# Differential attention scores as 96-row single-pass products, stacked by GpSimd's DMA queue

## What is computed

```
proj = einsum('bsd,de->bse', h, w_in[l])
q = proj[..., :512].reshape(B, S, 8, 2, 32)      # 8 heads, 2 components c, 32 wide
k = proj[..., 512:1024].reshape(B, S, 8, 2, 32)
s = einsum('bqhcd,bkhcd->bhcqk', q, k) * 32 ** -0.5 - slope[h] * |i - j|
p = softmax(s, axis=-1)
a = p[:, :, 0] - lam * p[:, :, 1]
o = einsum('bhqk,bkhd->bqhd', a, v)              # then normed, gained, projected by w_o
```

## Time and profile before

| | us |
|---|---|
| median of 3 runs | 933.48 |
| lowest and highest | 933.23, 933.65 |
| span of the profiled execution (first to last instruction) | 931.5 |
| attention stage, layer 0, from the first side piece to the last PV product of the heads | 366.6 to 419.8 |
| the same, layer 1 | 660.0 to 713.2 |

### The profile page before, as it was taken

The page is one execution under the profiler, slowest core; times in us unless marked ns, Lnnn a source line. Parts: engine busy times, 40 slices in busy tenths (PEclk is TensorE's granted clock), DMA queues, the critical chain, the costliest instruction groups (busy, mean ns, idle before and its releaser), DMA issues.

```text
span 931.5 us, 13488 instructions
## 1 busy us (share of the span) xinstructions
PE 910.4 (98%) x4978; PEld 766.7 (82%) x4978; DVE 606.7 (65%) x1071; ACT 473.2 (51%) x764; POOL 123.3 (13%) x100
## 2 busy tenths in 40 slices
PE   9999999999999999999999999999999999999996
PEld 6999878889888869887888888877978788888885
DVE  4898677676768586767664545567486965545445
ACT  5855757466686444762543443424574354334430
POOL 5643863102000010002000000000001100000001
PEclk9999999999999999999999999999999999999998
DMA  9655232663533118232475555444432265455521
GB/s 354 229 183 169 95 126 86 220 232 137 185 132 136 57 61 346 91 115 112 158 260 181 181 197 201 172 154 158 160 136 91 96 228 214 174 192 180 186 85 45
DMA packets 22235, 151.72 MB, mean 163 GB/s; under 512 B 2592, under 2 KB 2976, under 8 KB 4256
## 3 DMA queue, kind: packets, MB, share of 16 engines
q1 hardware_dynamic: 20160, 142.62, 42.6%
q10 hardware_dynamic: 2016, 8.29, 2.5%
HBM read 149.85 MB, written 1.05 MB: 162 GB/s over the span
## 4 chain that ended last, share of the span: by engine, by line
PE 86%; DVE 7%; issue 2%; ACT 2%; POOL 1%; DMA 1%; POOLq 0%; DVEq 0%; ACTq 0%; SPq 0%
PE ps L492 15%; PE ps L494 15%; PE ps L498 15%; PE ps L1091 5%; PE ps L523 3%; PE ps L527 3%; PE ps L525 3%; PE ps L767 2%; PE ps L769 2%; PE ps L768 2%; PE ps L543 2%; PE ps L663 2%; PE ps L1109 2%; PE ps L666 1%; PE ps L665 1%
## 5 line engine op out<-in xcount | busy, mean ns | idle before, releaser
L1275 ACT CAST whi<-raw 128x2048 fp32r<-128x2048 f32 (+1 forms) x127 | 241.2, 1906 | 146.1 <-PE ps L498 112.5
L1740 DVE TENSOR_TENSOR wlo<-raw,whi 128x1024 fp32r<-128x1024 f32 x127 | 166.9, 1314 | 139.9 <-ACT whi L1275 139.4
L492 PE MATMUL ps<-whi,ahi 128*128 128x512 f32 (+2 forms) x448 | 173.6, 387 | 0.9 <-issue 0.6
L494 PE MATMUL ps<-wlo,ahi 128*128 128x512 f32 (+2 forms) x448 | 171.7, 383 | 0.0
L498 PE MATMUL ps<-whi,alo 128*128 128x512 f32 (+2 forms) x448 | 170.7, 384 | 0.0
L1746 DVE TENSOR_TENSOR wlo<-raw,whi 128x1024 fp32r<-128x1024 f32 x106 | 129.2, 1219 | 0.0
L492 PEld LDWEIGHTS ps<-whi,ahi 128*128 128x128 f32 x448 | 84.1, 188 | 18.5 <-issue 2.5
L494 PEld LDWEIGHTS ps<-wlo,ahi 128*128 128x128 f32 x448 | 84.2, 188 | 16.4 <-issue 0.5
L498 PEld LDWEIGHTS ps<-whi,alo 128*128 128x128 f32 x448 | 84.1, 188 | 16.4
L523 PE MATMUL ps<-ahi,whi 128*128 128x256 f32 x256 | 73.2, 286 | 0.0
L525 PE MATMUL ps<-alo,whi 128*128 128x256 f32 x256 | 72.4, 283 | 0.0
(11 more groups left out here) (282 smaller groups left out, 1708.8 us busy)
## 6 DMA issues: line engine op xcount, KB each, us to landing
raw<-in_wstream SPq DMA_DIRECT2D x134, 1024.0 KB, 4.8
par<-in_params ACTq DMA_DIRECT2D x5, 1024.0 KB, 4.7
tab<-in_tables ACTq DMA_DIRECT2D x1, 1370.0 KB, 9.5
res<-in_x SPq DMA_DIRECT2D x2, 512.0 KB, 4.5
out<-res SPq DMA_DIRECT2D x4, 256.0 KB, 2.0
par<-in_params ACTq DMA_DIRECT2D x1, 512.0 KB, 3.6
arena<-in_wf ACTq DMA_DIRECT2D x2, 256.0 KB, 5.1
arena<-in_wsmall ACTq DMA_DIRECT2D x1, 256.0 KB, 8.5
```

Source lines behind the costliest of these rows:

```text
L492: pe.matmul(banks[b][:, 0:cw], h_, wh[:, i, c], start=st, stop=False, skip_group_check=True)
L494: pe.matmul(banks[b][:, 0:cw], h_, wl[:, i, c], start=False, stop=False, skip_group_check=True)
L1275: act.copy(whi[:, u % SPL, c], raw[:, u % RAW, c]).then_inc(w_hi, 1)
L1740: dve.tensor_tensor(wlo[:, u % SPL, c], raw[:, u % RAW, c], whi[:, u % SPL, c].bitcast(F32), ALU.subtract).then_inc(w_lo_v, 1)
```

## The change

Each of the four bank images of queries and keys is now kept as a high part and a low part, both in the arena: ACT writes the high part as fp32r (`qk_out`, one instruction each instead of two for queries), and DVE the low part, bank minus high part (`qk_lo`, new, 128x512, four per layer). POOL then issues three DMAs per head (`stack_head`, new) which put three 32-row blocks on top of each other in a ring buffer of three places: rows 0 to 31 high queries and high keys, rows 32 to 63 low queries and high keys, rows 64 to 95 high queries and low keys. One product of 96 rows in fp32r then gives all three terms, so a head has four single-pass products and no float32 ones. The three places are the first half of `bhi`, the first half of `blo`, and `wst`, all idle then.

The order moves as well: the first scores come after 16 side pieces instead of 3, and `side_pieces` becomes 20, 26, 32 for h = -1, 0, 1 where it was 12, 22, 32. On DVE the split of the unit `vu 2` moves behind `qk_lo(2)`, `qk_lo(1)` goes behind `combine(0)`, and `qk_lo(3)` behind `combine(1)`. A bank is free for the next pieces only after its low part too (`qk_done` is now counted by DVE). Scores of component 0 are handed to DVE before those of component 1 are made, and each bank has its own wait. The columns of the weights are put in another order on the host, as are the scales.

```diff
-    return (0, 12, 22, 32, 36, 40, 44)[h + 2] if h < 5 else 48
+    return (0, 20, 26, 32, 36, 40, 44)[h + 2] if h < 5 else 48
+FIRST_SCORES = 16
+STACKED = ((0, 0), (1, 0), (0, 1))
+RING = 3
...
                 def diff_scores(h):
                     if h == 0:
-                        pe.wait_ge(qk_done, 4 * l + 2)
                         pe.wait_ge(cw_done, 3 * l + 3)
-                    if h == NH // 2:
-                        pe.wait_ge(qk_done, 4 * l + 4)
-                    if h >= 1:
-                        pe.wait_ge(ds_max, 2 * NH * l + 2 * h)
-                    for t in range(T):
-                        for c in range(2):
-                            n = 2 * h + c
-                            rr = slice(n % 4 * HD, (n % 4 + 1) * HD)
-                            mm = pe.matmul(X[c][:, t * S:(t + 1) * S],
-                                           qkt[rr, n // 4, t * P:(t + 1) * P], qkt[rr, 4 + n // 4, :],
+                    pe.wait_ge(stacked[h % RING], stack_uses(l, h))
+                    rows_ = slice(0, HD * len(STACKED))
+                    q_, k_ = (stack[h % RING][rows_, s, :, :] for s in range(2))
+                    for c in range(2):
+                        if h >= 1:
+                            pe.wait_ge(ds_max, 2 * NH * l + 2 * h - 1 + c)
+                        for t in range(T):
+                            mm = pe.matmul(X[c][:, t * S:(t + 1) * S], q_[:, c, t * P:(t + 1) * P], k_[:, c, :],
                                            start=True, stop=True, skip_group_check=True)
-                            if t == T - 1:
-                                mm.then_inc(ds_psum, 1)
+                        mm.then_inc(ds_psum, 1)
...
-                for n in range(3):
+                for n in range(FIRST_SCORES):
                     side_piece(n)
                 diff_scores(0)
...
-                for i in QK_ORDER[:2]:
-                    split.until(("qk", l, i))
+                def qk_lo(i):
+                    j = QK_ORDER.index(i)
+                    dve.wait_ge(qk_hi, 4 * l + j + 1)
+                    bank, hi, lo = G[j % 2], qk_part(i, 0), qk_part(i, 1).bitcast(F32R)
+                    if i < 2:
+                        ins = dve.scalar_tensor_tensor(lo, bank, const("q_scale")[:, i:i + 1], hi, ALU.mult,
+                                                       ALU.subtract)
+                    else:
+                        ins = dve.tensor_tensor(lo, bank, hi, ALU.subtract)
+                    ins.then_inc(qk_done, 1)
+                split.until(("qk", l, 0))
+                qk_lo(0)
+                qk_lo(2)
+                split.until(("qk", l, 2))
...
                         combine(h)
-
+                    if h == 0:
+                        qk_lo(1)
+                    if h == 1:
+                        qk_lo(3)
...
+            def stack_head(l, h):
+                if h == 0:
+                    pool.wait_ge(qk_done, 4 * l + 2)
+                if h == NH // 2:
+                    pool.wait_ge(qk_done, 4 * l + 4)
+                if h >= RING:
+                    pool.wait_ge(ds_psum, 2 * NH * l + 2 * (h - RING) + 2)
+                m, at_ = h % 4, qks_at[h // 4]
+                for b, (fq, fk) in enumerate(STACKED):
+                    first, step_ = 512 * fq, 1024 + 512 * (fk - fq)
+                    src = arena[m * HD:(m + 1) * HD, at_ + first:at_ + first + 2 * step_]
+                    pool.dma_start(stack[h % RING][b * HD:(b + 1) * HD, :, :, :].rearrange("p s c t -> p s (c t)"),
+                                   src.rearrange("p (s x) -> p s x", s=2)[:, :, 0:512]
+                                   ).then_inc(stacked[h % RING], 16)
```

More of the change, by code:

```diff
@@ L193 @@
                   ("cos_s", T * S), ("sin_s", T * S), ("cos_c", P), ("nsin_c", P), ("inv", HR),
-                  ("q_scale", 4), ("ident2", 32)):
+                  ("q_scale", 2), ("ident2", 32)):
     TAB[_name] = (TAB_W, TAB_W + _w)
@@ L254, in build, with qk_part @@
         FB = [G[0], G[1], X[0], X[1]]
+        def qk_part(i, low):
+            at_ = qks_at[i % 2] + (2 * (i // 2) + low) * 512
+            return arena[:, at_:at_ + 512]
         def acc_bank(n, t, b):
@@ L330, in build @@
         rtmp = arena[:, 12800:13312]
-        qkt = arena[:, 0:2048].rearrange("p (k c) -> p k c", k=8)
+        qks_at = (0, 10240)
+        stack = [s_.rearrange("p k c -> p (k c)").rearrange("p (s c t) -> p s c t", s=2, c=2)
+                 for s_ in (bhi[:, 0:4, :], blo[:, 0:4, :], wst[:, :, :])]
         v2 = arena[:, 2048:3072].rearrange("p (t c) -> p t c", t=T)
@@ L388, in build @@
         r_final = sem("r_final")
-        qk_done, v_done, u_done = (sem("qk_done"), sem("v_done"), sem("u_done"))
+        qk_hi, qk_done, v_done, u_done = sem("qk_hi"), sem("qk_done"), sem("v_done"), sem("u_done")
+        stacked = [sem(f"stacked{r}") for r in range(RING)]
         ds_psum, ds_max, dp_done, da_done = sem("ds_psum"), sem("ds_max"), sem("dp_done"), sem("da_done")
@@ L399, in build, with stack_uses @@
         out_sent = sem("out_sent")
+        def stack_uses(l, h):
+            return 16 * len(STACKED) * (l * len(range(h % RING, NH, RING)) + h // RING + 1)
         block = ctx.enter_context(nc.Block())
@@ L1157, in diff_pv @@
                     mm.then_inc(do_psum, 1)
-                for n in range(3):
+                for n in range(FIRST_SCORES):
                     side_piece(n)
                 diff_scores(0)
-                for n in range(3, side_pieces(-1)):
+                for n in range(FIRST_SCORES, side_pieces(-1)):
                     side_piece(n)
@@ L1617, in qk_out @@
                     bank = G[QK_ORDER.index(i) % 2]
+                    dst = qk_part(i, 0).bitcast(F32R)
                     if i < 2:
-                        for j in range(2):
-                            ins = act.activation(qkt[:, 2 * i + j, :], bank[:, j * S:(j + 1) * S], ACT.Identity,
-                                                 scale=const("q_scale")[:, 2 * i + j:2 * i + j + 1])
-                    else:
-                        ins = act.copy(qkt[:, 2 * i:2 * i + 2, :], bank.rearrange("p (k c) -> p k c", k=2))
-                    ins.then_inc(qk_done, 1)
+                        ins = act.activation(dst, bank, ACT.Identity, scale=const("q_scale")[:, i:i + 1])
+                    else:
+                        ins = act.copy(dst, bank)
+                    ins.then_inc(qk_hi, 1)
                 split.until(("qk", l, 0))
@@ L2522, in _ @@
                 root_ln(0, (t,))
+            def stack_head(l, h):
[12 more added lines that the diff above has]
+                                   ).then_inc(stacked[h % RING], 16)
             for l in range(DEPTH):
+                for h in range(NH):
+                    stack_head(l, h)
                 for t in range(T):
@@ L2558, in shape_tables @@
     put("dist", np.concatenate([-HD ** 0.5 * np.abs(t * P + i[:, None] - k[None, :]) for t in range(T)], 1))
-    put("q_scale", 2.0 ** (2 * np.arange(4)[None, :] + 1 + i[:, None] // (2 * HD)))
+    put("q_scale", 2.0 ** (4 * np.arange(2)[None, :] + 1 + i[:, None] // HD))
     w = 2 * np.pi * np.outer(k, k) / S
@@ L2606 @@
         elif kind == "qk":
-            a = tiles(g["w_in_2"][name[1]], 0, 8, 256 * i, 256)
+            a = tiles(g["w_in_2"][name[1]], 0, 8, 256 * i, 256).reshape(P, 8, 4, 2, HD)
+            a = a.transpose(0, 1, 3, 2, 4).reshape(P, UW)
         elif kind == "vu":
```

## The result

The changed kernel takes 950.74 us (median of 4 runs, 950.12 to 951.93) against 933.49 for the kernel before beside it: ratio 1.0188, 95% interval 1.0176 to 1.0200, **slower by 17.3 us** where 932.3 was forecast. It is also outside the range of 930.5 to 939.0. All times here are medians without slow executions; the only one left out is one of the ten of run 6, at 1113.05 us.

The account below looks back on a forecast made before the run. TensorE, 98% busy, bounds the kernel; its 12.5 us saving mostly becomes waiting on the DVE/ACT chain. Per layer 0.5 - 1.1 = -0.6, twice -1.2: 933.48 becomes 932.3 us; own range 930.9 to 934.0, overall 930.5 to 939.0.

Parts of the forecast that it names:

- TensorE saves 0.78 per head: Scores on TensorE: four single-pass products take 0.72 us instead of 1.50; over 16 heads 12.5 us, the most possible.
- rival 2: TensorE's saving arrives: 12.5 us less the 0.65 waits reaches the end, about 921 to 925 us; chance 0.14.
- Copies and low parts: Before the first scores: ACT's high copy of a bank takes 0.59 us, DVE's low part 0.69.
- Issue on GpSimd: POOL's price for issuing one stacking DMA: 1.0 us, with ends 0.43 and 1.65; three per head.
- Rival 1: POOL's issues pace the stage, from about 1.15 us each; at 1.3, +3.0 us, 936.5 in all; chance 0.24.
- The estimate of 2.3 us: Skill page's price for one stacking DMA on POOL's queue, issue included; by it the lower end, -2.5 us.
- Landing, 1.8 us taken: Time from issue to landing of a 128 KB stacking DMA: 1.8 us, ends 1.5 and 4.8.
- The split of `vu 2`: Later on DVE, 368.1 to 370.4, hidden in its wait for first scores; costs nothing, 2.3 us without that cover.
- The chain through VectorE and ScalarE: Softmax rounds and u copies set the stage: first Fourier product 0.5 us later, layer 0.6 us shorter in all.
- rival 3: TensorE's clock falls to 1.2 GHz behind new idle stretches: +2.3 us per layer, 937; chance 0.08.
- The chances: Forecast 0.54 against three rivals with chances, a fourth given nothing; faster 0.34, same 0.34, slower 0.32.
- The end of 4.8 us: Upper end for a stack's landing: 3 us more at stack 0 and at stack 4, +10 in all.

Follow-up runs that it names:

- run 6: Changed kernel, with SyncE's weight loads held until the stacks of heads 2, 6 and 7 have landed: 934.40 us, ratio 1.0010 to the kernel before.
- Run 10: The kernel of run 5 with U's copy moved ahead, one more weight piece split before the scores, side pieces and load order changed: 923.08 us, ratio 0.9891.
- Run 4: Changed kernel with VectorE's split of `vu 2` put back ahead of `qk_lo(2)`: 943.18 us, ratio 1.0119 to the kernel before.
- run 2: Changed kernel without the 48 stacking transfers and the waits for them, scores reading whatever lies in the ring: 933.93 us, ratio 1.0007.
- run 5: Changed kernel with its stacking transfers unconverted and issued by SyncE, in one queue and ordered with its weight loads: 933.54 us, ratio 1.0000.
- run 8: Changed kernel with 12 and 8 useless products (layers 0 and 1) keeping TensorE busy before stack 1: 948.70 us, ratio 1.0161.
- run 12: Changed kernel on GpSimd's queue with weight loads held (behind stacks 2, 3, 7) and the moves of run 10: 926.89 us, ratio 0.9927.

## Why the prediction was wrong, by its own steps

- **TensorE saves 0.78 per head: right.** 1.50 us before, 0.73 around scores 2 against the 0.72 taken. Run 10 shows most of the 12.5 us of rival 2 arriving, but not in the changed kernel.
- **Copies and low parts: right.** 0.59 and 0.69 us as taken for the keys; for the queries 0.68 and 0.75, a little more.
- **Issue on GpSimd, 1.0 us taken: mis-sized.** It is 0.53 (medians of the three groups 0.527 to 0.537), in the lower part of the ends 0.43 to 1.65. Rival 1 (GpSimd paces from 1.15 us on) is thereby wrong, although the time ended on its side. The estimate of 2.3 us for one transfer with its issue, by the page "DMA: Bandwidth & Descriptors" of the Trainium skill (section "Anatomy of one DMA — SWDGE (gpsimd) path"), is near the 2.6 that a first stack took; run 6 has 3.1 to 3.6 with several in flight, and beside a load the rule falls short of the 7 to 10 us.
- **Landing, 1.8 us taken, ends 1.5 and 4.8: the step that failed.** Scores 0 started at 373.04, as forecast, but by luck: the first issue came at 368.93 instead of 368.19, the three took 1.8 us instead of 3.0, and stack 0 landed 2.2 us after the last of them instead of 1.8. From the fourth transfer on the time from issue to landing was 6.5 to 10.1 us, and up to 15.3 in the later bursts. I had taken rows of large transfers and a slope by bytes, and for the load beside it 0.3 us. The share of 0.34 is a mean over a stage in which loads come in bursts, and of the 6.3 MB I asked only whether they fit into that mean, not what the engines need for twelve transfers in a row (7.3 us) nor who is served first beside a load.
- **The split of `vu 2`: the second half of the same mistake.** I costed its move at nothing, because VectorE had idle time for it. It has; but the split frees `raw`, SyncE's load hangs on it, and so the load moved from ahead of the stacks into them. Run 4 puts 7.6 us on this.
- **The chain through VectorE and ScalarE: right, and shown without the transfers.** Maxima of head 3 at 387.55 forecast and 387.01 in run 2; first Fourier product at 405.5, and 405.01 in run 2, 405.29 in run 6, 405.03 in run 5. Scores 4 at 390.2, and 389.45 in run 6, which is the changed kernel without the overlap. In the changed kernel itself they came at 395.86, since stack 1's delay had already moved both low parts. One sum in this chain is short by 0.15 us (379.9 with 1.8, 1.99, 0.48 and 0.59 gives 384.76, not 384.6); nothing hangs on it.
- **The clock falls (rival 3): it did, and it should not have been a rival but a term.** In the changed kernel it followed from the waits for stacks, and what run 8 took away of it was worth about 2 us. But runs 2, 5 and 6 show it with no stack late beyond 2.7 us: 1.2 us per layer in run 5, where rival 3 had 2.3. Run 6, the changed kernel without the overlap, is 2.1 us above the forecast, and in it too the window behind the first Fourier product has the clock at 0.90.
- **The chances.** All four cases were drawn from the same steady landing, so the range could not hold a collision. The end of 4.8 us was in the sum, at +10, and I cut the range at 939 below it.

The size, from the profiles: the forecast had TensorE work 12.5 us less in a time 1.2 us shorter, so wait 11.3 us more. It waited 19.7 us more, 18.8 of them for stacks, and was busy only 2.9 us less. The three stretches at the half clock hold 15.1 us of its busy time, of which half, 7.6, is an estimate of what the clock added; without it most of that would have been more waiting, as run 8 shows. About 2 us of busy time are left that I can't place.

## What to carry to other kernels

Where an edit adds transfers, add up what the 16 DMA engines need for the burst, by the packets and not by the bytes of a larger transfer, and look which loads an edit moves: a step that frees a buffer is also the start of the next load, however well the step itself is hidden. An average share of the DMA engines says nothing of a burst. And a gain on the busiest engine arrives only when the engines half a microsecond behind it are relieved too: here neither half was worth 2 us, both together 10.

## What the runs showed of the hardware

- Beside one load of 1 MB from SyncE's queue (8 KB packets), the transfers of GpSimd's queue (packets of about 2 KB) got 11.0% of the DMA engines' time for four microseconds against 79.6%; the load, for its part, took 10.5 us instead of 4.8. Together they needed 12.3 us of all engines for what their prices alone put at 9.9.
- Transfers of 128 KB between places of SBUF move at 208 GB/s with the engines at 96.7%, weight loads at 320 GB/s with 79.6%.
- GpSimd issues one in 0.53 us, whether it converts or not. After eleven issues within 6 us it stood still for 5.72 us in layer 0, while loads ran (in layer 1 twelve issues within 6 us went out without that, so the number alone is not the reason):

```profile
396.90 1.03 POOL L2564 DMA_DIRECT2D blo<-arena  x2
403.65 0.53 POOL L2564 DMA_DIRECT2D blo<-arena  x1 [5.72 <-issue]
```

  What it waited for the trace does not say; scores 7 did not wait for it.
- The clock went to the lower of its two levels, 1.2 GHz, for 6.8 us at a time behind waits of 5.6 and 4.1 us. The length of the last wait does not tell it: in run 4 it fell for 6.8 us at a wait of 2.6 us, in run 12 for 3.4 us behind one of 2.0, and in run 2 for 3.4 us some 1.6 us after the end of a wait of 1.4. In run 10, with no stack wait above 0.9 us, it stayed at 2.4 GHz through both stages.
